# Down-projection loads of the experts moved from SyncE's queue to ScalarE's, behind a copy that ScalarE makes

## The reference

```python
def moe(x, router_w, router_b, w_gate, w_up, w_down):
    ...
    _, idx = lax.top_k(jnp.where(in_grp, sel, -jnp.inf), TOP_K)          # 2 of 16 experts per token
    ...
    hid = jax.nn.silu(jnp.einsum('bld,edf->blef', x, w_gate)) * jnp.einsum('bld,edf->blef', x, w_up)
    hid = hid * comb[..., None].astype(hid.dtype)
    return jnp.einsum('blef,efd->bld', hid, w_down)
```

## Time and profile before

| | us |
|---|---|
| three runs | 1054.91, 1048.94, 1054.9 |
| their median | 1054.9 |
| the profiled execution, its own time | 1050.59 |
| its span, first to last instruction | 1048.9 |
| DMA, bytes over the span | 277.51 MB, mean 265 GB/s |

### The profile page before, as it was taken

The page is one execution under the profiler, slowest core; times in us unless marked ns, Lnnn a source line. Parts: engine busy times, 40 slices in busy tenths (PEclk is TensorE's granted clock), DMA queues, the critical chain, the costliest instruction groups (busy, mean ns, idle before and its releaser), DMA issues.

```text
span 1048.9 us, 11959 instructions
## 1 busy us (share of the span) xinstructions
PE 932.7 (89%) x4772; PEld 519.5 (50%) x4772; DVE 408.1 (39%) x829; ACT 175.7 (17%) x309; POOL 226.1 (22%) x334
## 2 busy tenths in 40 slices
PE   6999988998984799999989569989937999999993
PEld 4888867984343233333333259954324333333331
DVE  3799318634546022212224275612262111111115
ACT  0401221223010111111011252211111111110101
POOL 4679962201412411111000200000012111100000
PEclk9999987998996899999999985569968999999997
DMA  9356639002749579999999824372097799999982
GB/s 262 97 187 248 236 129 292 1 12 98 250 149 411 220 299 396 411 409 397 401 415 422 361 62 151 115 256 82 1 391 288 300 363 407 402 400 402 419 358 83
DMA packets 83578, 277.51 MB, mean 265 GB/s; under 512 B 25337, under 2 KB 44231, under 8 KB 60854
## 3 DMA queue, kind: packets, MB, share of 16 engines
q1 hardware_dynamic: 70298, 255.86, 63.6%
q10 hardware_dynamic: 10660, 16.49, 4.9%
q0 software_dynamic: 2560, 4.33, 1.4%
HBM read 261.49 MB, written 18.01 MB: 266 GB/s over the span
## 4 chain that ended last, share of the span: by engine, by line
PE 74%; DMA 15%; DVE 5%; ACT 2%; issue 1%; ACTq 1%; POOL 0%; SPq 0%; POOLq 0%; DVEq 0%
PE ps L1756 18%; PE ps L320 11%; DMA ring<-in_moe_w_up 10%; PE ps L1780 8%; PE ps L2420 5%; PE ps L1798 4%; PE ps L1735 3%; PE ps L761 3%; PE ps L2298 2%; PE ps L2283 2%; DMA x_rows<-work 2%; PE ps L736 1%; DMA work<-in_ln_ffn_b 1%; PE ps L609 1%; PE ps L2296 1%
## 5 line engine op out<-in xcount | busy, mean ns | idle before, releaser
L1756 PE MATMUL ps<-ring,work 128*64 128x512 f32 x480 | 219.8, 610 | 9.5 <-DMA ring<-in_moe_w_up 8.1
L1757 PE MATMUL ps<-ring,work 128*64 128x512 f32 x480 | 219.9, 610 | 0.0
L1756 PEld LDWEIGHTS ps<-ring,work 128*64 128x64 f32 x480 | 64.3, 140 | 137.7 <-issue 122.8
L1840 DVE TENSOR_TENSOR work<-ps,work 64x512 f32<-64x512 f32 x32 | 33.8, 1055 | 223.5 <-ACT work L1811 223.5
L320 PE MATMUL ps<-work,ring 128*128 128x264 f32 x512 | 115.2, 387 | 0.0
L1780 PE MATMUL ps<-ring,work 128*64 128x512 f32 x248 | 113.0, 598 | 2.1 <-DVE work L1845 1.4
L1781 PE MATMUL ps<-ring,work 128*64 128x512 f32 x248 | 113.1, 598 | 0.0
L320 PEld LDWEIGHTS ps<-work,ring 128*128 128x128 f32 x512 | 96.8, 190 | 16.4
L1202 POOL TENSOR_TENSOR ring<-ring 128x512 f32<-128x512 f32 (+5 forms) x76 | 90.5, 1209 | 9.0 <-DVE ring L1198 5.7
L1850 DVE COPY work<-ps 64x512 f32<-64x512 f32 x32 | 22.2, 694 | 150.4 <-PE ps L1781 150.4
L1861 POOL COPY work<-work 64x1 int32<-64x1 int32 x32 | 5.7, 179 | 335.5 <-PE ps L1735 297.6
(11 more groups left out here) (494 smaller groups left out, 1266.1 us busy)
## 6 DMA issues: line engine op xcount, KB each, us to landing
ring<-in_moe_w_down SPq DMA_DIRECT2D x31, 2048.0 KB, 17.0
ring<-in_moe_w_gate SPq DMA_DIRECT2D x60, 1024.0 KB, 14.7
ring<-in_moe_w_up SPq DMA_DIRECT2D x60, 1024.0 KB, 16.8
ring<-in_w_in ACTq DMA_DIRECT2D x6, 2048.0 KB, 8.5
s_out_mats<-ring SPq DMA_DIRECT2D x4, 1280.0 KB, 4.7
ring<-in_w_in SPq DMA_DIRECT2D x2, 2048.0 KB, 10.3
s_in_mats<-ring SPq DMA_DIRECT2D x4, 1024.0 KB, 6.1
ring<-in_w_out SPq DMA_DIRECT2D x1, 4096.0 KB, 17.0
```

The costliest lines, as they stand in the source:

```text
L1756: nc.tensor.matmul(ps[0:SLOT, 5, :], xgT[s][:, c], gate_w[slot][:, c], start=c == 0, stop=c == DC - 1)
L1757: last = nc.tensor.matmul(ps[SLOT:P, 5, :], xgT[s][:, c], up_w[slot][:, c], start=c == 0, stop=c == DC - 1)
L1840: nc.vector.tensor_tensor(hid[s][0:SLOT].rearrange("t (c p) -> t p c", c=4), strided(ps[SLOT:P, 5, :]), strided(sg[s][SLOT:P]), ALU.mult). ...
```

## The change

The down loads of the list in `moe_weights` are taken out of it. They are issued by ScalarE in `moe_act`, each right behind the copy of the previous expert's result (`act_y`): in the first stage, behind the copy for expert k - 1 the down weights of k + 1, for k = 1 to 14. In the second stage, where there are three places, behind the copies for experts 0 and 1 those of experts 3 and 4, behind that for expert 2 none, and from the copy for expert 3 on again those of k + 1. `down_load` itself, with its wait for `down_done`, is the same. The first loads ahead of the loop and those of the further rounds stay on SP. So SP's list has gate and up alone from expert 3 on.

```diff
@@ moe_act
                 if k > 0:
                     act_y(a, l, *at_expert(k - 1))
+                    freed = k + 2 if l == 1 and k < 3 else k + 1 if l == 0 or k > 3 else NE
+                    if freed < NE:
+                        down_load(a, l, *load_of(freed))
             act_y(a, l, *at_expert(NE - 1))
@@ moe_weights
             moe_first_loads(q, l)
             for k in range(3, NE):
                 gate_up_load(q, l, *load_of(k))
-                if (l, k) != (1, 3):
-                    down_load(q, l, *load_of(k - 1))
-            down_load(q, l, *load_of(NE - 1))
```

## The result

The changed kernel takes 1063.87 us (median of 4 runs, 1062.97 to 1065.1), the kernel before 1051.93 (4 runs, 1048.94 to 1054.91): ratio 1.013, 95% interval 1.0096 to 1.0164. It is slower by 12 us between the two medians and by some 14 us by the ratio. The profiled execution has a span of 1063.4 us, 14.5 more than before. One execution of the kernel before, beside which the first experiments were run, took 2349 us; it counts as a slow one and is left out of all ratios.

A forecast was written before the change was run, and what follows sets the result against it. TensorE, 89% busy, was taken as the bound, waiting for expert weights at stage ends with DMA engines full. First stage +4, second +8, clock +1 gave +13 on 1050.6, 1063.6; 1066 for a median of new runs, range 1051 to 1077.

The forecast's parts named there:

- the second stage's overtaking: Late in the second stage, down loads on ScalarE's queue pass the gate-and-up load TensorE needs first: +8 us (4.8 to 9.6).
- the clock: After longer waits TensorE runs at half its granted clock for a stretch: +1 us (0 to +3.4).
- the full gain of the third rival: Idle DMA stretches used by earlier expert-4 loads pay in full, the 6.6 and 3.9 us waits go: 1040 us, chance 7%.
- The head start: First stage: gate-and-up 4 goes ahead of down 2, putting the DMA engines 3 us (2 to 4) ahead until TensorE's waits.
- The second stage's move: Down 4, no longer behind gate-and-up 5, fills part of the idle stretch 829 to 836.5 us: 0 us gained.
- ScalarE's half microsecond: Each down load issued behind a ScalarE copy goes out 0.5 us later, hidden by the DMA engines' backlog.
- Turns by packet, and the bigger packets win: Two queues alternate packet for packet, so 16.4 KB down packets get two thirds of the engines against 8.2 KB gate-and-up packets.
- The prediction's other case: By the Trainium skill, a down load goes through at one turn, in 7.2 us or less; gate-and-up still loses 4.8 us.
- GU15 overtaken by D14 and D15: End of second stage: down loads of experts 14 and 15 pass expert 15's gate-and-up load, delaying its landing to 1020.6 us.
- One overtaking alone: Rival: only expert 14's down load overtakes, expert 15's comes too late; both stages at lower bounds, 1057 us, chance 15%.
- The neutral split: Rival: two queues keep landings in order of need, only the head start is left, 1047.6 to 1050.6 us, chance 13%.
- the rival of dry engines behind a long wait: Waits of 8 us or more hold back the next gate-and-up load: 5 us more per stage, 1073 to 1080, chance 5%.

The follow-up runs named there:

- the run with the two moves alone: Against the kernel before, all loads on SP's queue, gate-and-up of expert 4 ahead of down 2 (first stage), down 4 ahead of gate-and-up 5 (second): 0.9987 (0.9966 to 1.0007).

## Why the prediction was right, point by point

The time (1063.87 us, 1066 forecast, +13 on the profiled execution, 14.5 there) and the mechanism were right. The terms were less so, and that they add up so well is in part luck: the second stage's overtaking was put some 4 us too high and the clock some 3 us too low. The 1066 also started from the median of three runs, 1054.9, which a fourth run brought down to 1051.93; as a ratio 1.0105 was forecast, and 1.013 measured.

*What TensorE waited for.* The 6.6 and 3.9 us without TensorE work at the ends of the stages were all read as waits for weights. The page of before has 8.1 us for w_up in both stages together: 4.3 in the first and 3.8 in the second. The rest of the first stage's 6.6 is other idle time, so the full gain of the third rival, down to 1040, was put too high. The sum does not use them.

*The head start.* Down 3 lands 7.9 us after its issue in the changed kernel too, in place of 12.4: 4.5 us on the DMA side, 3 forecast. What it is worth in time was put too high: the run with the two moves alone gained 1.4 us, with zero inside its interval. The premise that failed is that the head start is kept because the share stays at 1.01: from 385 to 410 us the share is 0.86 in the changed kernel, where it was 1.02. The second stage's move gave nothing that shows, as forecast.

*ScalarE's half microsecond.* There is none. The issue at 942.37 us is at the start of the copy (942.36), not behind its end. The sum had it hidden, so nothing hangs on it.

*Turns by packet, and the bigger packets win.* Right, and shown at three sizes. The prediction's other case, a down load that goes through at one turn, is not what the records show: it shares the engines row by row. D loads take 12 us where 10 were forecast, since the first packets come some 4 us after the issue (954.32, first ones at 958).

*The two stages.* First stage: ScalarE's first copy, which stands ahead of the first load issued there, is at 374.26 us against 372.99, so the profiled execution was 1.3 us late before anything of the change could tell. From there on every copy keeps that distance up to the wait at expert 9; the last copy is at 591.87 against 583.71. Cost of the stage: 8.2 - 1.3 = 6.9 us. Second stage: first gate product at 806.57 against 798.78, last combination at 1042.74 against 1028.22, so 14.5 - 7.8 = 6.7 us. The rows, first of before, then of the changed kernel:

```profile
372.99 0.58 ACT L1835 COPY work<-ps 64x512 f32<-64x512 f32 x1 [3.01 <-PE ps L1781]
...
798.78 0.64 PE L1756 MATMUL ps<-ring,work 128*64 128x512 f32 x1 [0.68 <-ACT work L1807]
...
1028.22 3.68 PE ps L1798 x8
```

```profile
374.26 0.58 ACT L1835 COPY work<-ps 64x512 f32<-64x512 f32 x1 [3.01 <-PE ps L1781]
...
591.87 0.47 ACT work L1835
...
806.57 0.64 PE L1756 MATMUL ps<-ring,work 128*64 128x512 f32 x1 [0.68 <-ACT work L1807]
...
1042.74 3.68 PE ps L1798 x8
```

1.3 + 6.9 - 0.4 (the part between the stages) + 6.7 is the 14.5 us of the spans. The 1.3 is thus not the change's. Both costs hold what half clock cost (below): 1.4 us more than before in the first stage, 2.7 in the second. Without it the first stage lost 5.5 us, where 4 was forecast (1.8 to 6.8), and the second 4.0, where 8 was forecast (4.8 to 9.6): below its range.

*Where in the stage.* This step of the second stage failed, and with it the size of its term. The prediction put the whole loss at the last load: GU15 overtaken by D14 and D15, landing last. The trace has it at expert 11, in one wait, and GU15 in time (its use has no wait: TensorE is busy for all 57 us from 975 on; its last up half lands at 1022.9, D15 at 1029.6). The reason is one that the prediction named only for its size: while TensorE stands for 7 us, the DMA engines go on, and what they gain is cover for the rest, since they fall behind slowly (the wait of before comes only at the stage's end). The working was right about how much an up half may be overtaken by, two down loads, and wrong about which one.

*The clock.* Behind the wait of 6.97 us the granted clock is 0.57 in the mean of 6.3 us, so 2 x 0.43 x 6.3 = 5.4 us at half speed, which cost 2.7; behind that of 7.00 us 2 x 0.14 x 10 = 2.8 us, which cost 1.4; and behind that of 2.23 us at expert 9 it is 0.51 for 3.5 us, so 3.4 us at half speed and 1.7 lost. Before, one stretch cost 1.7. So +4.1 us, above the 0 to 3.4 and four times the +1 taken. The second stage adds up: 8.2 us of waits from 940 us on and 2.7 of clock, less the 3.8 of waits it had, are 7.1, measured 6.7.

*The rivals.* One overtaking alone (1057) is excluded by the landing order of down 10, down 11 and up 11. The neutral split and the full gain are excluded by the ratio. Behind the long wait of the second stage the DMA engines run less than full (0.91 from 975 us on), and by then nothing needs them; the gaps from 385 to 410 us come before any wait. So the rival of dry engines behind a long wait did not decide.

## What to carry to other kernels

Where transfers on one queue stand in the order of need and the DMA engines fall behind, moving a part of them to another queue does not speed them up, it changes who pays. Here the queue with fewer bytes and larger packets was served at once, and all of the lag fell on the other; with small packets it was the down loads that came late. Ask which of the two has the cover for it, and keep no more places open for the favoured one than it needs. A load that lands 38 us before its use, while another comes 7 us late, is the sign to look for.

## What was not expected of the hardware

- A DMA issue that stands behind a copy in ScalarE's list goes out with the copy's start, 10 ns behind it (942.36 and 942.37 us), not after its 0.58 us. Nothing here depends on their order: the load waits for the same semaphore as the copy, not for the copy.
- Packets of two queues take turns one for one at 4, 8 and 16 KB beside 8 KB, within 6% (455 to 458, 167 to 176, 112 to 114), at 416 to 442 GB/s in all: the mix costs no rate. Sixteen packets of one queue start within 0.5 us, and then those of the other: with 16 KB rows a turn is one packet on each engine.
- Four down transfers of 512 KB in place of one of 2048 KB cost 5 us over 32 experts on one queue (1.0048, 1.0022 to 1.0074). Why stays open.
